# Expert results at the end of a MoE block: six of eight rows of a token packed two to a tile and added pairwise by TensorE

## What is computed

```python
def _moe(u, w_router, router_bias, we_gate, we_up, we_down, ws_gate, ws_up, ws_down):
    ...
    _, eidx = lax.top_k(sel, TOP_K)            # TOP_K = 8
    ...
        act = (jax.nn.silu(hg) * hu * gk[..., None]).astype(tk.dtype)
        return jnp.einsum('nef,efd->nd', act, we_down).astype(jnp.float32)
    ...
    return (routed + shared).reshape(B, S, D)
...
        ffn = _moe(u, w_router[l], router_bias[l], we_gate[l], we_up[l], we_down[l], ws_gate[l], ws_up[l], ws_down[l])
        x = _layer_norm(ALPHA * x.astype(jnp.float32) + g2[:, None, :] * ffn, ln2_g[l], ln2_b[l]).astype(dtype)
```

## Time and profile before

| | us |
|---|---|
| median of three runs | 1296.65 |
| the profiled execution | 1294.08 |
| its span, first to last instruction | 1292.4 |
| first load of results issued | 1229.98 |
| last matmul of the experts' items begins its group | 1238.50 |
| last of VectorE's instructions begins its group | 1288.48 |

### The profile page before, as it was taken

One profiled execution on the slowest core, in us unless ns is written; L12 is line 12 of the kernel. 1 busy time (PEld: TensorE's weight loads), 2 busy tenths in 40 slices (PEclk: granted clock), 3 DMA queues, 4 the chain that ended last, 5 costly groups with the idle time before them and its releaser, 6 DMA issues.

```text
span 1292.4 us, 22910 instructions
## 1 busy us (share of the span) xinstructions
PE 1258.3 (97%) x6355; PEld 723.2 (56%) x6355; DVE 833.8 (65%) x1773; ACT 750.2 (58%) x975; POOL 188.1 (15%) x371
## 2 busy tenths in 40 slices
PE   6999999999999999999999999999999999999995
PEld 6777788877777788875333433333333333333342
DVE  5837777667878555888465555555555555655578
ACT  4465552335454433134677777777777777777722
POOL 1000000000010100122112221221221222122100
PEclk9999999999999999999999999999999999999998
DMA  8833356579831551456879999999999999998395
GB/s 318 258 98 97 131 176 219 196 254 174 285 131 33 179 212 55 151 194 239 322 318 387 334 405 402 394 377 387 393 374 406 390 416 365 410 399 333 105 384 245
DMA packets 109523, 353.68 MB, mean 274 GB/s; under 512 B 18438, under 2 KB 57463, under 8 KB 83746
## 3 DMA queue, kind: packets, MB, share of 16 engines
q1 hardware_dynamic: 90562, 303.04, 63.4%
q0 software_dynamic: 18912, 50.01, 10.8%
HBM read 326.07 MB, written 47.20 MB: 289 GB/s over the span
## 4 chain that ended last, share of the span: by engine, by line
PE 85%; DVE 6%; DMA 5%; ACT 2%; issue 1%; SPq 1%; DVEq 0%; ACTq 0%
PE bank L1262 26%; PE bank L1287 13%; PE bank L904 9%; PE bank L906 9%; PE bank L905 9%; PE bank L1249 3%; DMA gu<-in_we_up 3%; PE bank L1272 2%; PE bank L1023 2%; PE bank L1047 1%; PE bank L1149 1%; DMA y_all<-y_rows 1%; PE bank L862 1%; PE bank L1119 1%; PE bank L1118 1%
## 5 line engine op out<-in xcount | busy, mean ns | idle before, releaser
L1262 PE MATMUL bank<-gu_use,x_t 128*64 128x512 f32 x1664 | 368.5, 595 | 0.0
L1635 ACT ACTIVATE gu_use<-gu 128x1024 f32 x208 | 209.1, 1058 | 56.0 <-PE bank L1262 31.6
L1262 PEld LDWEIGHTS bank<-gu_use,x_t 128*64 128x64 f32 x1664 | 114.9, 137 | 216.4 <-issue 216.2
L1628 ACT ACTIVATE down_use<-down 128x2048 f32 x103 | 190.9, 1902 | 0.0
L1287 PE MATMUL bank<-down_use,act_t 128*64 128x512 f32 x832 | 187.4, 592 | 0.0
L904 PE MATMUL bank<-h_hi,w_lo 128*128 128x512 f32 x424 | 170.7, 402 | 1.1 <-DVE w_lo L1787 1.1
L2319 DVE COPY gu_use<-gu 128x1024 f32 x208 | 132.9, 691 | 53.2 <-PE bank L1262 38.4
L906 PE MATMUL bank<-h_hi,w_hi 128*128 128x512 f32 x424 | 165.6, 391 | 0.0
L905 PE MATMUL bank<-h_lo,w_hi 128*128 128x512 f32 x424 | 165.3, 390 | 0.0
L1787 DVE TENSOR_TENSOR w_lo<-stream,w_hi 128x1024 fp32r<-128x1024 f32 x71 | 86.8, 1222 | 94.9 <-ACT w_hi L1383 94.8
L2285 DVE TENSOR_TENSOR pick<-slot_id,places 128x512 bf16<-128x512 f32 x53 | 36.7, 693 | 145.0 <-POOL columns L811 145.0
(11 more groups left out here) (362 smaller groups left out, 1737.3 us busy)
## 6 DMA issues: line engine op xcount, KB each, us to landing
gu<-in_we_gate SPq DMA_DIRECT2D x64, 1024.0 KB
gu<-in_we_up SPq DMA_DIRECT2D x64, 1024.0 KB, 9.1
down<-in_we_down SPq DMA_DIRECT2D x64, 1024.0 KB, 8.5
stream<-in_w_in SPq DMA_DIRECT2D x28, 1024.0 KB, 7.1
ada_w<-in_w_ada POOLq DMA_DIRECT2D x8, 2048.0 KB, 9.9
y_rows<-zeros SPq DMA_DIRECT2D x8, 2048.0 KB, 12.5
y_all<-y_rows SPq DMA_DIRECT2D x7, 2048.0 KB, 15.8
ada_first<-in_w_ada SPq DMA_DIRECT2D x16, 512.0 KB, 11.0
```

The lines of the kernel that those rows point to most:

```text
L1262: last = nc.tensor.matmul(bank[item.par][rows, :], x_t[:, k, rows], gu_use[h][:, :, k, :], start=(k == 0), stop=(k == KD - 1))
L1628: nc.scalar.activation(down_use[h][:, :, :], down[:, bass.ds(slot, 1), :, :].rearrange("p o k n -> p (o k) n"), ACT.Copy).then_inc(down_ta ...
L1635: return nc.scalar.activation(gu_use[h][:, 1, ks, :], gu[:, bass.ds(slot, 1), 1, ks, :].rearrange("p o k n -> p (o k) n"), ACT.Copy)
```

## The change

Of the eight ranks of a tile, ranks 0 to 5 are now added by TensorE and ranks 6 and 7 by VectorE.

- **Layout.** For ranks 0 to 5, two ranks share the 128 partitions: partitions 0 to 63 hold one rank and 64 to 127 another, and the tile's tokens 0 to 63 and 64 to 127 (c = 0, 1) stand behind each other in the free direction. So each such load writes 64 partitions alone, and there are two (`part` 0 and 1) where there was one. The even slot takes ranks 0 to 3 (two loads of 1 MB), the odd slot ranks 6 and 7 as before, a token to a partition (one load of 1 MB), and ranks 4 and 5 (two loads of 0.5 MB). A load moves pieces of 8 KB where two ranks of a token lie side by side and of 4 KB for ranks 4 and 5; before, a piece was 16 KB.
- **TensorE.** `stack` is 128x64, two identities of 64 on top of each other. A matmul of `stack` against 128x512 adds two ranks of 64 tokens; c = 0 and c = 1 write the lower and the upper 64 partitions of the same PSUM bank, one after the other in the program. In tile 3 `sum_last` comes ahead of the ranks, then six matmuls of `ones` whose result nobody reads, and the ranks close the sum.
- **VectorE.** It adds two ranks instead of five (tile 3: instead of four), and `norm_out(2)` now stands ahead of `sum_in(3)`. One small instruction makes `stack`, some 780 us earlier, in the token mixer's stage.
- **Waits.** A tile's loads of tiles 2 and 3 wait together for both counts. For tile 3 ranks 6 and 7 are loaded first.

```diff
-BY_PE = 3
...
+        stack = at("stack", 2, [P, P // 2])
...
-            for n in range(2 * NT):
-                if n == 3:
+            def ranks_of(t):
+                return y_rows[t * P * TOPK:(t + 1) * P * TOPK, :]
+            def load_pairs(t, slot, pairs, first, count):
+                by_half = ranks_of(t).rearrange("(c q k) d -> q c k d", c=2, k=TOPK)
+                to = y_all[slot][:, 0:2 * pairs, :].rearrange("p (c g) d -> p c g d", c=2)
+                for part in range(2):
+                    ranks = slice(first + part * pairs, first + (part + 1) * pairs)
+                    sp.dma_start(to[part * P // 2:(part + 1) * P // 2, :, :, :], by_half[:, :, ranks, :]).then_inc(count, 16)
+            def load_rows(t, slot, count):
+                by_token = ranks_of(t).rearrange("(p k) d -> p k d", k=TOPK)
+                sp.dma_start(y_all[slot][:, 2:4, :], by_token[:, TOPK - 2:TOPK, :]).then_inc(count, 16)
+            for t in range(NT):
+                even, odd = 2 * t % 4, 2 * t % 4 + 1
+                if t >= 2:
+                    sp.wait_ge(rows_summed, t - 1)
+                    sp.wait_ge(rest_read, t - 1)
+                if t == NT - 1:
+                    load_rows(t, odd, y_end_in)
+                load_pairs(t, even, 2, 0, y_in[even])
+                if t == 1:
                     sp.wait_ge(gu_half, pairs * 4)
                     sp.wait_ge(route_ready, 1)
-                if n >= 4:
-                    sp.wait_ge(rest_read, n - 3)
-                if n in (4, 6):
-                    sp.wait_ge(rows_summed, n // 2 - 1)
-                results = y_rows[n // 2 * P * TOPK:(n // 2 + 1) * P * TOPK, :].rearrange("(p k) d -> p k d", k=TOPK)
-                first = n % 2 * TOPK // 2
-                if n < 2 * NT - 1:
-                    sp.dma_start(y_all[n % 4][:, :, :], results[:, first:first + TOPK // 2, :]).then_inc(y_in[n % 4], 16)
-                else:
-                    sp.dma_start(y_all[n % 4][:, 0:2, :], results[:, first:first + 2, :]).then_inc(y_in[n % 4], 16)
-                    sp.dma_start(y_all[n % 4][:, 2:4, :], results[:, first + 2:first + 4, :]).then_inc(y_end_in, 16)
-                if n == 3:
+                if t < NT - 1:
+                    load_rows(t, odd, y_in[odd])
+                load_pairs(t, odd, 1, 4, y_in[odd])
+                if t == 1:
                     sp.dma_start(ln2g_row[:, :], ln2_g.partition_broadcast(P)).then_inc(ln2_in, 16)
...
-            def sum_rows(t, half):
+            def sum_pairs(t, slot, pairs, half, ends=False):
                 o, cols = sums(t, half)
-                for k in range(BY_PE if t < NT - 1 else TOPK // 2):
-                    last = nc.tensor.matmul(o, ident[:, :], y_all[2 * t % 4][:, k, cols], start=(t < EARLY and k == 0),
-                                            stop=False)
-                if half:
+                rows = y_all[slot][:, 0:2 * pairs, :].rearrange("p (c g) d -> p c g d", c=2)
+                for g in range(pairs):
+                    for c in range(2):
+                        last = nc.tensor.matmul(o[c * P // 2:(c + 1) * P // 2, :], stack[:, :], rows[:, c, g, cols],
+                                                start=(t < EARLY and pairs == 2 and g == 0), stop=ends)
+                return last
+            def sum_even(t):
+                slot = 2 * t % 4
+                pe.wait_ge(y_in[slot], 32 * (t // 2 + 1))
+                for half in range(2):
+                    sum_pairs(t, slot, 2, half)
+            def sum_odd(t, ends=False):
+                slot = 2 * t % 4 + 1
+                pe.wait_ge(y_in[slot], 48 * (t // 2 + 1) - (16 if t == NT - 1 else 0))
+                for half in range(2):
+                    last = sum_pairs(t, slot, 1, half, ends)
+                    if ends:
+                        last.then_inc(first_summed, 1)
+                if not ends:
                     last.then_inc(rows_summed, 1)
-            def sum_last(t, half):
+            def sum_last(t, half, ends=True):
                 o, cols = sums(t, half)
                 for s in range(2):
                     for part in (y_lo, y_hi):
                         last = nc.tensor.matmul(o, spot[s][:, t * P:(t + 1) * P], part[s][:, cols], start=False,
-                                                stop=(s == 1 and part is y_hi))
-                last.then_inc(first_summed, 1)
+                                                stop=(ends and s == 1 and part is y_hi))
+                if ends:
+                    last.then_inc(first_summed, 1)
-            for t in range(NT):
+            for t in range(NT - 1):
+                sum_even(t)
                 if t == 2:
                     sum_shared(3)
-                pe.wait_ge(y_in[2 * t % 4], 16 * (2 * t // 4 + 1))
-                for half in range(2):
-                    sum_rows(t, half)
+                sum_odd(t)
                 if t == 0:
                     pe.wait_ge(spot_ready, 2)
                     pe.wait_ge(y_lo_ready, Y_PARTS + 2)
                 for half in range(2):
                     sum_last(t, half)
+            for half in range(2):
+                sum_last(NT - 1, half, False)
+            for _ in range(6):
+                nc.tensor.matmul(bank[6][:, 0:P], ones[:, :], ones[:, :], start=True, stop=True)
+            sum_even(NT - 1)
+            sum_odd(NT - 1, True)
...
+                V.tensor_tensor(stack[:, :], ident[:, 0:P // 2], ident[:, P // 2:P], ALU.add)
...
-            def add_first(t):
-                rows = x1[:, t, :]
-                dve.wait_ge(y_in[2 * t % 4], 16 * (2 * t // 4 + 1))
+            def add_rows(t):
+                rows, slot = x1[:, t, :], 2 * t % 4 + 1
+                if t < NT - 1:
+                    dve.wait_ge(y_in[slot], 48 * (t // 2 + 1))
+                else:
+                    dve.wait_ge(y_end_in, Y_END + 16)
                 if t < EARLY:
-                    last = V.tensor_tensor(rows, rows, y_all[2 * t % 4][:, BY_PE, :], ALU.add)
+                    link(V.tensor_tensor(rows, rows, y_all[slot][:, 2, :], ALU.add))
                 else:
-                    last = V.scalar_tensor_tensor(out=rows, in0=rows, scalar=ALPHA, in1=y_all[2 * t % 4][:, BY_PE, :],
-                                                  op0=ALU.mult, op1=ALU.add)
-                last.then_inc(rest_read, 1)
-                dve.wait_ge(rest_read, 2 * t + 1)
-            def add_rest(t, first, last_k):
-                rows = x1[:, t, :]
-                dve.wait_ge(y_in[2 * t % 4 + 1], 16 * (2 * t // 4 + 1))
-                for k in range(first, last_k):
-                    if t == NT - 1 and k == 2:
-                        dve.wait_ge(y_end_in, Y_END + 16)
-                    if t == NT - 1 and k == 0:
-                        last = V.scalar_tensor_tensor(out=rows, in0=rows, scalar=ALPHA, in1=y_all[2 * t % 4 + 1][:, k, :],
-                                                      op0=ALU.mult, op1=ALU.add)
-                    else:
-                        last = V.tensor_tensor(rows, rows, y_all[2 * t % 4 + 1][:, k, :], ALU.add)
-                    if k < TOPK // 2 - 1:
-                        link(last)
-                if last_k == TOPK // 2:
-                    last.then_inc(rest_read, 1)
-                    dve.wait_ge(rest_read, 2 * t + (2 if t < NT - 1 else 1))
+                    link(V.scalar_tensor_tensor(out=rows, in0=rows, scalar=ALPHA, in1=y_all[slot][:, 2, :], op0=ALU.mult,
+                                                op1=ALU.add))
+                V.tensor_tensor(rows, rows, y_all[slot][:, 3, :], ALU.add).then_inc(rest_read, 1)
+                dve.wait_ge(rest_read, t + 1)
...
-            add_first(0)
             result_out(last_item)
-            add_rest(0, 0, 1)
+            add_rows(0)
             result_low(1)
-            add_rest(0, 1, TOPK // 2)
             for t in range(NT - 1):
                 sum_in(t)
-                if t + 1 < NT - 1:
-                    add_first(t + 1)
-                    add_rest(t + 1, 0, 2)
-                    variance(t)
-                    add_rest(t + 1, 2, TOPK // 2)
-                    norm_out(t)
-            add_rest(NT - 1, 0, 2)
-            variance(NT - 2)
-            add_rest(NT - 1, 2, TOPK // 2)
+                add_rows(t + 1)
+                variance(t)
+                norm_out(t)
             sum_in(NT - 1)
             variance(NT - 1)
-            norm_out(NT - 2)
             norm_out(NT - 1)
```

## The result

| | before | after |
|---|---|---|
| median, us | 1295.87 (4 runs) | 1327.14 (4 runs, 1326.31 to 1328.03) |
| the profiled execution | 1294.08 | 1326.43 |
| its span | 1292.4 | 1324.6 |

The ratio is 1.0248, with a 95% interval of 1.0233 to 1.0263: the change makes the kernel 2.5% slower, 31 us. The direction was forecast. The size was too small: span +32.2 us against +22.8.

A forecast was written before the change was run, and what follows sets the result against it. Loads bound the kernel before 1266 and VectorE after; with the change, loads decide. Last landing 1304.8 + 1.1 + 9.3 = 1315.2 against 1292.4: +22.8, added to median 1296.65 gives 1319.4 us, range 1290 to 1328.

The forecast's parts named there:

- The rate of the halves, 214 GB/s: Result loads writing 64 partitions: 12.6 MB at half the full rate take 58.8 us instead of 29.4; chance 0.57.
- The first 2 MB: Sign in the profile: first pair of result loads lands at 1242.8 at half rate, against 1237.9 before.
- The last landing, 1304.8: End of the result loads: moves from 1275.4 to 1304.8, +29.4 us, with the halves at 214 GB/s.
- TensorE, 1.1 us behind the last landing: Tile 3: four counts for half of ranks 4 and 5, 0.9 us, plus 0.2 until VectorE sees them.
- the clock: TensorE ahead of tile 3's matmuls: idling may lower the granted clock, costing 0 to 1.5 us; taken as 0.
- VectorE's last stretch, 9.3 us: From VectorE's reading of tile 3's sums to the end: 12.05 us less 2.77 for norm_out(2) moved ahead.
- the three rows of its waits: Sign in the profile: VectorE waits for loads and PSUM 30 to 40 us in all instead of 3.7.
- SyncE's issues, `stack`: 0: 20 issues instead of 9, about 0.45 us each, hidden behind the stream; the instruction making `stack` 0 to 0.2, taken 0.
- Half-width matmuls at half the time: TensorE's rank sums: 0.222 us a count against 0.45 full-width, so a tile's 24 counts take 5.3 us.
- rival 3: TensorE's half-width pairs run one after the other, loads at full rate: -0.5 us; chance 0.05 shared with rates 260 to 428.
- Rival 1: Half-partition loads run at full rate: last landing 1275.9, end 1287.6, -4.8 us, median 1291.8; chance 0.33.

The follow-up runs named there:

- The mixture: The kernel before, with loads of even slots cut into lower and upper halves of the partitions, odd slots left at 128 partitions; 1320.03 us, span 1318.3.

## Why the prediction was wrong

The direction and the mechanism were right: the loads decide it, and their rate is halved. The sizes fell short by 9.4 us of span, in two terms.

- **The rate of the halves, 214 GB/s.** Right: 209 and 210 GB/s where only halves are under way. To read the 177 GB/s of the earlier trace rows as a half of 350 gave the right value, but with some luck: the packets there were also far smaller than those behind the 350, and that row alone could not tell the two apart (the 291 GB/s of small packets beside it spoke for the halves, but with other packets mixed in). The first 2 MB were forecast for 1242.8 and came at 1241.9, with the first issue 1 us earlier.
- **The last landing, 1304.8.** This step failed: 1310.85, though the first issue was 1.0 us earlier, so the stream was 7.1 us longer than the sum. The sum changed the rate of the 12.6 MB and left the other 4.2 MB, the four full loads that now stand between halves, at 428 GB/s. They did not keep that rate. Cutting them into halves too cost 1.6 us where the sum has 9.8, so by this reading they had lost 8.2 us, enough for the whole miss. The mixture gives less: 1 us for each 2 MB load behind halves; and in the changed kernel itself the first full load, 1 MB, lands at 1230.31 + 15.0 = 1245.3, 3.4 us behind the half ahead of it, where 2.45 were due. At 1 us for each of the four it would be 4 of the 7.1 us. Which of the two readings holds, and why a full load is slowed there, is open. The sum also lacks the stores of finished tiles. Two of them landed within the longer stream (1277.28 + 32.2 = 1309.5 and 1299.8 + 10.9 = 1310.7), and in before both came in behind the last load (1276.5 and 1278.0). With them held back the stream was 3.8 us shorter, but the lead arose before they moved (above), so it is not shown that they are a part of the miss.
- **TensorE, 1.1 us behind the last landing.** This step failed too: 4.5 us. Most of the miss is the clock. I took 0 of 0 to 1.5 us, because ranks 0 to 3 should come in time to absorb it; it cost 2.4 us (6.86 against 4.47 for the 20 counts). The other 1.0 us is that they did not come in time. I had them 4.9 us ahead of the last load. The chain has the second load of the pair landing at 1308.44, 2.4 us ahead, and from there the 20 counts take 4.5 us even at the full clock, so they end 2.1 us behind the last landing instead of 1.1.
- **VectorE's last stretch, 9.3 us.** Right, 9.2. What it sheds brought nothing here; the three rows of its waits above are 44.7 us, where 30 to 40 were forecast.
- **SyncE's issues, `stack`: 0.** Right: most issues of a half take 0.6 us, and in stretches of 4 us from 1234 to 1310 the DMA share never falls below 0.97.
- **Half-width matmuls at half the time.** Right, 0.228 a count, so rival 3 was wrong on its premise.
- **Rival 1**, the full rate, happened in the kernels whose loads reach both halves. Its last landing, 1275.9, was right to 0.1 us, but by luck: the first issue was 1.3 us earlier than in before, and the stream of 47.2 us as much longer than forecast (45.9). Its -4.8 was not right: span 1290.4, -2.0, because TensorE reached tile 3 only at 1276.65. I had left out tile 3's shared expert, 3.7 us of matmuls in the middle of tile 2, and the slow clock of the group ahead of it (5.2 us for 16 counts instead of 3.65). Moving the shared expert gave 3.0 us back: from the first issue to the end that kernel is 3.7 us shorter than before, still 1.1 short of the 4.8.

In numbers: the span's +32.2 is -1.0 for the earlier start, +36.4 of stream, and -3.2 behind the last landing (13.8 us to the end instead of 17.0). Over the forecast's +22.8 it is 7.1 of stream, -1.0 of start, +3.4 of TensorE and -0.1 of VectorE, so 9.4. The forecast was added to the median of 1296.65, and on that the ratio of 1.0248 gives 1328.8, just beyond the end of the range at 1328. What carried the result there are the 7.1 us of stream, for which the rate of the full loads that I had left as it was is the cause best supported here, and the 2.4 us of the clock, which I had put at 0.

## What to carry to other kernels

Before packing two things into the partition axis, ask which partitions each load writes: a load that stays in 0 to 63 or in 64 to 127 costs twice the time at a full DMA share, and the same packing with alternating partitions costs nothing. Loads to all partitions that stand between such loads don't keep their full rate either (6.0 us instead of 4.9 for 2 MB here, and perhaps more), so a sum that changes only the terms of the halves comes out too small. And where TensorE idles longer ahead of its last matmuls, price them at the lower clock: here 6.97 us of idle time went before 20 counts that took 6.86 us instead of 4.47.

## What the runs showed of the hardware

- Half of the partitions is not one thing: 0 to 63 or 64 to 127 gave 210 GB/s, every second one 414. The DMA share reads 1.0 in both, so a busy share alone doesn't tell that a stream runs at half its rate.
- A full load of 2 MB behind halves took 6.0 us instead of 4.9, in the mixture. In the changed kernel four full loads of 1 MB saved 1.6 us in all over halves, where 9.8 would be due.
- Loads of the two halves from two queues overlap in part (stream 71.7 us instead of 81.9); from one queue, one behind the other, hardly: in the kernel before with all loads as halves the first six, 1 MB each, landed 5.0 us apart.
- The part ahead of 1229, in which the kernels here differ by one small instruction at most, ended 3 to 5 us later in three of the profiled executions (first issue at 1232.09, 1233.42 and 1233.69). These were compared by their streams, not by their spans. Why it ends later is open.
